# Storing the normed tokens in the order of the weight rows

## What is computed

```python
for i in range(2):
    hl = xl * (1 + sc1) + sh1
    yl = diff_attention(hl, ctx) if i == 0 else pool_mixer(hl)
    xl = layer_norm(ALPHA * xl + (1 + g1) * yl, ln_g[i, 0], ln_b[i, 0])
    tokens = xl * (1 + sc2) + sh2
    y2 = moe_ffn(tokens, router_w, router_b, wg[i], wu[i], wd[i])   # top 2 of 16 experts
    xl = layer_norm(ALPHA * xl + (1 + g2) * y2, ln_g[i, 1], ln_b[i, 1])
```

## Time and profile before

| | us |
|---|---|
| median of 3 runs | 1341.49 |
| lowest and highest | 1334.39 and 1345.14 |
| the profiled execution, its own time | 1343.82 |
| its span on the core | 1341.9 |
| PE busy | 1229.0 (92%) |
| mean granted TensorE clock | 0.971 |

### The profile page before, as it was taken

The page is one execution under the profiler, slowest core; times in us unless marked ns, Lnnn a source line. Parts: engine busy times, 40 slices in busy tenths (PEclk is TensorE's granted clock), DMA queues, the critical chain, the costliest instruction groups (busy, mean ns, idle before and its releaser), DMA issues.

```text
span 1341.9 us, 12310 instructions
## 1 busy us (share of the span) xinstructions
PE 1229.0 (92%) x5261; PEld 564.1 (42%) x5261; DVE 379.3 (28%) x781; ACT 166.5 (12%) x398; POOL 23.0 (2%) x28
## 2 busy tenths in 40 slices
PE   5999999988999999999999998899999999999996
PEld 1444344454644434444443435644444444444332
DVE  1486897854211111111111113311111111111103
ACT  0200123332201000000100002400100000010000
POOL 0011001000000000000000010000000000000000
PEclk8799899899899999999999999999999999999997
DMA  9668867606899999999999998299999999999950
GB/s 330 260 251 316 318 238 255 251 1 247 344 418 423 426 429 429 427 426 428 429 426 428 428 420 369 95 420 422 427 427 428 428 428 427 427 428 427 428 236 32
DMA packets 54924, 476.27 MB, mean 355 GB/s; under 512 B 5018, under 2 KB 6442, under 8 KB 30292
## 3 DMA queue, kind: packets, MB, share of 16 engines
q1 hardware_dynamic: 42632, 433.04, 77.3%
q0 software_dynamic: 10560, 41.94, 8.5%
q10 hardware_dynamic: 1676, 0.46, 0.3%
HBM read 474.38 MB, written 1.05 MB: 354 GB/s over the span
## 4 chain that ended last, share of the span: by engine, by line
PE 81%; DVE 10%; DMA 4%; issue 2%; ACT 2%; SPq 0%; DVEq 0%
PE ps L731 50%; PE ps L723 9%; PE ps L528 5%; PE ps L739 5%; DMA ring<-in_mod_w 4%; DVE modp L1150 3%; PE ps L593 2%; DVE work L1480 2%; DVE work L1484 2%; PE ps L747 1%; PE ps L557 1%; PE ps L501 1%; PE ps L575 1%; PE ps L682 1%; PE ps L451 1%
## 5 line engine op out<-in xcount | busy, mean ns | idle before, releaser
L731 PE MATMUL ps<-ring,tra 128*64 128x512 f32 x2048 | 446.5, 594 | 1.1 <-ACT tra L1032 1.1
L731 PEld LDWEIGHTS ps<-ring,tra 128*64 128x64 f32 x2048 | 146.1, 137 | 296.6 <-issue 295.1
L731 PE MATMUL ps<-ring,work 128*64 128x512 f32 x1024 | 228.5, 598 | 29.5 <-DVE work L1480 29.5
L731 PEld LDWEIGHTS ps<-ring,work 128*64 128x64 f32 x1024 | 83.3, 137 | 154.1 <-issue 117.9
L528 PE MATMUL ps<-ring 128*128 128x512 f32 x320 | 142.7, 599 | 0.7 <-ACT ring L921 0.7
L723 PEld LDWEIGHTS ps<-extra,xn 128*128 128x128 f32 x512 | 121.7, 328 | 25.7 <-issue 22.7
L723 PE MATMUL ps<-extra,xn 128*128 128x128 f32 x512 | 127.5, 405 | 2.7 <-DVE extra L1389 2.7
L1150 DVE SCALAR_TENSOR_TENSOR modp<-ring,modp 128x512 f32<-128x512 f32 x140 | 105.3, 752 | 5.0
L1475 DVE TENSOR_TENSOR work<-ps,work 128x512 f32<-128x512 f32 x32 | 22.1, 692 | 283.4 <-ACT work L1039 283.4
L528 PEld LDWEIGHTS ps<-ring 128*128 128x128 f32 x320 | 59.8, 192 | 78.1 <-issue 77.1
L739 PE MATMUL ps<-work,extra 64*128 64x512 f32 x256 | 63.6, 615 | 25.1 <-DVE work L1484 25.1
(11 more groups left out here) (177 smaller groups left out, 641.5 us busy)
## 6 DMA issues: line engine op xcount, KB each, us to landing
ring<-in_moe_wg SPq DMA_DIRECT2D x64, 2048.0 KB, 14.8
ring<-in_moe_wu SPq DMA_DIRECT2D x64, 2048.0 KB, 12.1
ring<-in_moe_wd SPq DMA_DIRECT2D x64, 2048.0 KB, 12.1
ring<-in_mod_w POOLq DMA_DIRECT2D x20, 2048.0 KB, 9.7
ring<-in_attn_wqkv SPq DMA_DIRECT2D x6, 2048.0 KB, 15.0
ring<-in_mod_w SPq DMA_DIRECT2D x4, 2048.0 KB, 18.6
ring<-in_attn_wo SPq DMA_DIRECT2D x2, 2048.0 KB, 9.0
xn<-in_x SPq DMA_DIRECT2D x1, 1024.0 KB, 17.0
```

The lines of the kernel that those rows point to most:

```text
L731: last = mm(ps[SLOTS * h:SLOTS * h + SLOTS, b, :], lhs(k0 + k), w[:, k, h * NB:(h + 1) * NB], start=(k0 + k == 0), stop=(k0 + k == KT - 1) ...
```

## The change

The normed tokens for norms 0 and 2 are stored in `xn` in the order of a unit's weight rows (`in_order`): within a half, all features 4f come first, then 4f + 1, and so on. A gather then reads 128 neighbouring columns. What else follows:

- norm 0 can't be done in place; the residual sum goes to `zbuf`, a piece of the ring's slot of unit 7, so SP's load of unit 7 waits for the norm instead of the sum;
- router weights are loaded in two transfers in the second order, and `bcol`, `acol`, `xcol` for the router and the residual use index 1;
- `open_sums` in the router (start=True) writes its 128 columns to every fourth column of the bank, which brings the sums back to the natural order; the one in the pool layer stays as it was;
- `route` on PE gets fillers: three after the second of its four turned parts and one after the last.

```diff
+        zbuf = [ring[:, e9:e9 + D], small9]
+        def in_order(n, to, src):
+            if n == 1:
+                return to, src
+            return to.rearrange("p (k f) -> p f k", k=4), src.rearrange("p (f k) -> p f k", k=4)
...
                 elif v == 7:
-                    sp.wait_ge(sem("gated"), 2 * TT)
+                    normed(sp, 0, 1)
...
             def open_sums(t, k, start):
-                return mm(bank(2 * t + k // 4, 0, P, k % 4 * P, k % 4 * P + P), xT8[:, k, t * P:t * P + P], ident,
-                          start=start and k % 4 == 0, stop=True, skip_group_check=True)
+                to = bank(2 * t + k // 4)
+                to = to.rearrange("p (f k) -> p k f", k=4) if start else to.rearrange("p (k f) -> p k f", k=4)
+                return mm(to[:, k % 4, :], xT8[:, k, t * P:t * P + P], ident, start=start and k % 4 == 0, stop=True,
+                          skip_group_check=True)
...
                     turn_blocks(NT_BANK[part], xn[:, t * D + b * NB:t * D + (b + 1) * NB]).then_inc(sem("nT_done"), 1)
+                    if part == 1:
+                        keep_clock(NT_BANK[2], 3)
+                keep_clock(0, 1)
...
-                        half = xn[:, t * D + b * NB:t * D + (b + 1) * NB].rearrange("p (f k) -> p k f", k=4)
-                        last = mm(bank(bk, 0, P, k * P, k * P + slots), half[:, k, :], sgat[:, t, 0:slots],
+                        c0 = t * D + b * NB + k * P
+                        last = mm(bank(bk, 0, P, k * P, k * P + slots), xn[:, c0:c0 + P], sgat[:, t, 0:slots],
...
-            load(rw[:, :].rearrange("p (k n) -> p k n", k=KT)[:, :, 0:NE], router_w.rearrange("(k p) n -> p k n", p=P), "router_loaded")
+            for b in range(2):
+                load(rw[:, P * b:P * b + P].rearrange("p (k n) -> p k n", k=4)[:, :, 0:NE],
+                     router_w[HALF * b:HALF * b + HALF, :].rearrange("(p k) n -> p k n", p=P), "router_loaded")
...
-                half = xn[:, t * D + h * NB:t * D + (h + 1) * NB]
-                nc.scalar.activation(half, half if n == 0 else bank(2 * t + h), ACT.Identity, bias=m_[:, 4:5],
-                                     scale=m_[:, 2:3]).then_inc(sem("norm_act"), 1)
+                src = zbuf[t][:, h * NB:(h + 1) * NB] if n == 0 else bank(2 * t + h)
+                to, src = in_order(n, xn[:, t * D + h * NB:t * D + (h + 1) * NB], src)
+                nc.scalar.activation(to, src, ACT.Identity, bias=m_[:, 4:5], scale=m_[:, 2:3]).then_inc(sem("norm_act"), 1)
```

More of the change, by code:

```diff
@@ L636, in job @@
                     pe.wait_ge(sem("cols_ready"), 1)
-                    pe.wait_ge(sem("router_loaded"), 32)
+                    pe.wait_ge(sem("router_loaded"), 48)
                     for layer in range(DEPTH):
@@ L640, in job @@
                             last = mm(bank(bk, 0, P, NE * layer, NE * layer + NE),
-                                      one(bcol[2 * layer], k).to_broadcast([P, P]), rw[:, 32 * k:32 * k + NE],
+                                      one(bcol[2 * layer], k, 1).to_broadcast([P, P]), rw[:, 32 * k:32 * k + NE],
                                       start=(k == 0), stop=(k == KT - 1), skip_group_check=True)
@@ L1255, in job_out @@
                         link(v_.tensor_tensor(bcol[n], bcol[n], sh_, ALU.add))
-                        v_.tensor_scalar(xcol[:, 0, n], g[:, 0], ALPHA, None, ALU.mult)
-                        link(v_.tensor_scalar(xcol[:, 1, n], b[:, 0], ALPHA, None, ALU.mult))
+                        s_ = 0 if n == 1 else 1
+                        v_.tensor_scalar(xcol[:, 0, n], g[:, s_], ALPHA, None, ALU.mult)
+                        link(v_.tensor_scalar(xcol[:, 1, n], b[:, s_], ALPHA, None, ALU.mult))
                     v_.tensor_scalar(flat, bcol[1][:, 0].rearrange("p q h -> p h q"), cst[:, C_FLAT:C_FLAT + 1], None,
                                      ALU.mult).then_inc(sem("cols_ready"), 1)
-                    dve.wait_ge(sem("router_loaded"), 32)
+                    dve.wait_ge(sem("router_loaded"), 48)
                     scaled_router(0)
                 else:
-                    dve.wait_ge(sem("router_loaded"), 32)
+                    dve.wait_ge(sem("router_loaded"), 48)
                     v_.tensor_tensor(rb[:, NE:3 * NE].rearrange("p (l e) -> p l e", l=2),
@@ L1271, in scaled_router @@
                 four = lambda a: a[:, :].rearrange("p (h q n) -> p h q n", h=2, q=4)
-                a_ = acol[2 * layer][:, 0].rearrange("p q h -> p h q").unsqueeze(3).to_broadcast([P, 2, 4, 32])
+                a_ = acol[2 * layer][:, 1].rearrange("p q h -> p h q").unsqueeze(3).to_broadcast([P, 2, 4, 32])
                 v_.tensor_tensor(four(rwa[layer]), four(rw), a_, ALU.mult).then_inc(sem("rw_ready"), 1)
@@ L1327, in norm @@
                 dve.wait_ge(sem("rstd_ready"), TT * n + 2)
-                v_.tensor_scalar(xn[:, D + NB:2 * D], src, m_[:, 0:1], m_[:, 2:3], ALU.subtract, ALU.mult)\
+                to, src = in_order(n, xn[:, D + NB:2 * D], src)
+                v_.tensor_scalar(to, src, m_[:, 0:1], m_[:, 2:3], ALU.subtract, ALU.mult)\
                     .then_inc(sem("norm_dve"), 1)
@@ L1335, in attention_norm @@
                         c0, c1 = h * NB, (h + 1) * NB
-                        z, y = xn[:, t * D + c0:t * D + c1], ybuf[:, c0:c1]
+                        x_, z, y = xn[:, t * D + c0:t * D + c1], zbuf[t][:, c0:c1], ybuf[:, c0:c1]
                         mixed(dve, t, h)
                         link(v_.tensor_tensor(y, bank(2 * t + h), gate1[:, c0:c1], ALU.mult))
-                        ins = v_.scalar_tensor_tensor(out=z, in0=z, scalar=ALPHA, in1=y, op0=ALU.mult, op1=ALU.add)
+                        ins = v_.scalar_tensor_tensor(out=z, in0=x_, scalar=ALPHA, in1=y, op0=ALU.mult, op1=ALU.add)
                         ins.then_inc(sem("gated"), 1)
@@ L1344, in attention_norm @@
                     deviation(0, t)
-                norm(0, xn[:, D + NB:2 * D])
+                norm(0, zbuf[1][:, NB:D])
             def sums_norm(n, ready):
```

## The result

The changed kernel takes 1288.6 us (median of four runs, 1287.9 to 1292.7) against 1343.2 us for the kernel before: a ratio of 0.961 [0.956, 0.966]. The prediction was 1284, with a range of 1272 to 1295. The same kernel, run again beside the last experiments, gave 1287.1 us (six runs, 1280.1 to 1291.2) and 0.959 [0.955, 0.962].

The account below looks back on a forecast made before the run. PE's chain of 29.32 us an expert was taken as the bound, with transfers 24 us a layer behind. PE alone would gain 60.3 us; waits for units cut this to 56.7, from 1341.5 to 1284, range 1272 to 1295.

Parts of the forecast that it names:

- router of layer 0, the clock: From logits to first gather in layer 0, added fillers keep the clock up: 2.6 us saved.
- half-gathers, 14 a layer: Half-gathers in the expert loop read contiguous weights at 118 ns each: 1.89 us instead of 3.93, 28.6 us a layer.
- first gathers, both layers: First gather of each layer, 32 instructions reading contiguous weights, about half at low clock: 2.5 us saved a layer.
- strided PSUM write, both: Residual sums in each router write PSUM with a step of four, at 213 ns each: 1.8 us lost a layer.
- norms, both: Norms stored with a step of 512 bytes slow ACT's halves: 0.3 us lost a layer, bounds nothing to 0.6.
- fillers in layer 1: In layer 1's router the added fillers delay PE, mostly hidden by ACT's table load: 0.3 us lost.
- waits for units, both layers: At each layer's end PE waits for its last ring unit: 1.5 us in layer 0, another 2.1 in layer 1.
- The transfers: Expert units land at 4.915 us each, 417.8 us for 85 a layer, using up the cushion, so both bounds meet.
- Rival 3: Expert unit transfers hold their old pace of 4.944 us or worse: 1289, or 1297 at 4.99; chance 0.12.
- Rival 5: Gathers get no faster, the address step not being the cause; clock and small costs remain: 1343; chance 0.05.
- Rival 6: In the expert loop PE's clock falls once it waits for weights: 1390 with five such experts; chance 0.03.
- Rival 4: Everything falls well: 111 ns gathers, warm first gathers, free PSUM writes, transfers at 4.89 us: 1273; chance 0.05.

Follow-up runs that it names:

- the control: The changed kernel run again with no edit: 1287.1 us (six runs), ratio 0.959 to the kernel before.
- experiment 2: The changed kernel without its added fillers: 1286.1 us (four runs), ratio 0.960 to the kernel before.
- experiment 3: The changed kernel with half of each expert unit loaded and the matmuls reading that half twice: 1281.8 us, ratio 0.954.
- experiment 10: The changed kernel again; with more fillers ahead of first gathers; and also with norms reordered on the read and attention fillers: 1287.1, 1281.1, 1280.0 us.
- experiment 5: The changed kernel with gathers reading their weights at a step of two fp32 values instead of one: 1284.6 us (one run).
- experiment 7: The changed kernel with open_sums in the pool layer too writing every fourth PSUM column: 1290.0 us (one run).
- experiment 8: The changed kernel with norms reading at a step of 16 bytes and storing in order, instead of storing at 512: 1290.2 us (one run).
- experiment 9: The kernel before with half the bytes of the expert weights loaded and each read twice by the matmuls: 1342.3 us (one run).
- experiment 4: The changed kernel gathering only one of the four blocks of features: 1282.3 us (four runs), ratio 0.956.
- experiment 6: The changed kernel with gathers reading their weights at a step of eight fp32 values instead of one: 1341.2 us (one run).
- the last version of experiment 10: The changed kernel with more router fillers, norms reordered on the read and three fillers in the attention: 1280.0 us (six runs), ratio 0.953.

## Why the prediction was right

The time was off by 4.6 us and the gain from the projection on by 0.3. The second is closer than its terms, of which some were off in both directions. Term by term, in us of gain (before to after, from the rows above and those of before):

| step | predicted | measured |
|---|---|---|
| router of layer 0, the clock | 2.6 | 2.6 |
| half-gathers, 14 a layer | 28.6 twice | 27.3 twice |
| first gathers, both layers | 5.0 | 1.05 + 1.2 = 2.3 |
| strided PSUM write, both | -3.6 | 0 |
| norms, both | -0.6 | -0.45 twice = -0.9 |
| fillers in layer 1 | -0.3 | -0.3 |
| waits for units, both layers | -3.6 | -1.5 - 1.2 = -2.7 |
| last down matmuls | 0 | 1.5 |
| sum | 56.7 | 57.1 (by the spans 57.0) |

**Half-gathers.** The mechanism was right, the price wrong by 6 ns: 124 ns an instruction, the higher of the two rows it was taken between the earlier trace rows, so 3.93 - 1.98 = 1.95 us each instead of 2.04. The row nearer in kind was the band matmuls, which read the same tile.

**First gathers.** These were over-priced. The prediction let half of each run cold; after, both ran nearly whole at 0.50, and their 6.70 and 6.54 us are close to the 6.8 us that it had worked out for that case. A window within layer 0's:

```profile
348.00:350.00 2.00, 2.00 (x11) 2.00 (x11) 0.61 (x6) 0.00 (x0) 0.00 (x0) 0.50 1.02 434
```

Other executions had 5.2 to 5.5 us in one layer or both (the control above, experiments 2 and 3), so half warm is seen too, and 3.84 in layer 1 of experiment 2. Experiment 10 takes what is left. The prediction let the clock in the first gather be as before, and priced the fillers for the stretch ahead of it only. In six traces with these fillers and no more (the changed kernel's two, experiments 3, 5, 7 and 8) both first gathers took over 5 us, and in the one trace without them layer 1's took 3.84. So the fillers may have a cost there that the sum doesn't have; one trace doesn't show it.

**The router's clock.** In layer 0 the added fillers did what the sum had them do. The logits of layer 0 take 1.11 us, in the chain after, where they took 1.98, and from them to the first gather it is 347.65 - 337.91 = 9.74 us instead of 12.33. In layer 1 it was 9.74 before and is 9.70 now. Their price there was right too: from layer 0's last scatter to layer 1's logits it is 28.65 us before, 29.10 without the fillers (experiment 2) and 29.40 with them. So 0.45 us are the norm's and 0.3 the fillers'.

**PSUM write.** Priced at 1.8 us a layer between bounds of 0 and 2.9; the lower bound is the truth (experiment 7). In layer 1, in the changed kernel, the 32 of them take the same 4.27 us as before:

```profile
821.58 4.27 PE L691 MATMUL ps<-cst,work 128*128 128x128 f32 x32
```

**Norms.** They cost 0.45 us a layer, between the 0.3 that was taken and the bound of 0.6: ACT's last half, which PE waits for, went from 0.8 us to 1.24 and 1.29 (experiment 8). In layer 0 this is the way from the projection to the logits, 20.57 us before and 21.04 after.

**The last down matmuls.** 7.26 us instead of 8.81, a gain of 1.5 us that no step foresaw. It isn't the change's: the kernel before had 7.11 in experiment 9, and the kernels of experiments 2 and 4, made from the changed one, had 8.78. The clock's fall there comes and goes between executions. Without it the gain in this pair of traces would have been 55.5 us.

**The transfers.** The step that decided the forecast held. The time of issue and the time to landing of layer 0's unit 10 (unit 95, issued at 745.4, is the 40.24 us in the chain above):

```profile
L356 SPq DMA_DIRECT2D ring<-in_moe_wd x1: 328/328/328, 358.8 to 358.8; - x1
DMA to landing us min/median/max: 7.7/7.7/7.7
```

Unit 10 lands at 366.5 and unit 95 at 785.65: 419.1 us for 85, 4.931 each. In layer 1 unit 107, issued at 840.3, lands 7.9 us later at 848.2, and unit 192, issued at 1226.8, lands 40.4 us later at 1267.2: 419.0 us, 4.929 each. The prediction had these four at 365.3, 783.1, 846.7 and 1264.5: each is 1.2 to 2.7 us later than that. But this execution reached its projection 1.5 us later than the one before (316.87 against 315.35); counted from there, they are within 0.3 us at the start of each layer, and 1.0 and 1.2 us late at its end. The forecast had 4.915, and the upper rival 4.944. PE lost 1.5 us in layer 0 and 1.2 in layer 1, against 1.5 and 2.1. These are the times by which the experts of a layer took longer than their own work; the idle times shown above are 1.04 and 1.03 us of them, and each break in a row of matmuls costs another 0.2 (two times sixteen take 3.65 + 3.65 us where 32 in a row take 7.09). **Rival 3** in its milder form is half true, at 0.015 us a unit.

Errors of some 6 us each way cancelled. The gathers gave 2.6 + 2.7 us less and the norms 0.3 less; the PSUM write, the last down matmuls and the waits gave 3.6 + 1.5 + 0.9 more. That the gain came out within 0.3 us is luck; that it lay near 57 is not. The prediction's structure also made it forgiving: where two bounds meet, an error on PE's side comes back in part as shorter or longer waits. Of the 4.6 us between 1284 and the median, 1.7 lie in the kernel before, whose median beside it was 1343.2 instead of 1341.5. The rest is that these medians differ by 54.7 us and the traces by 57.0 from the projection on; beside the control the medians differ by 56.4. That is within what executions differ by in their first 320 us (last section).

**Rival 5** (the step isn't the cause) is refuted by experiment 6, which puts the step back and with it the time. **Rival 6**, the fall of the clock in the expert loop, is seen inside the loop only in experiment 4 and decides nothing there; in a layer's last down matmuls it comes and goes in both kernels and costs 1.5 to 1.7 us each time. **Rival 4** asked for warm first gathers and free PSUM writes; experiment 10's versions have both and reach 1280, not 1273, for a gather's instruction takes 120 to 124 ns instead of 111 and the transfers stayed at 4.93 us a unit.

## What to carry to other kernels

When two places load weights of the same shape and one takes twice as long, compare their address steps: here fp32 weights cost 124 to 130 ns per 128 columns with at least two values in every 16 bytes and 246 to 250 with one, and the order of storing could be chosen for the reader, because only the norm, the router's weights and the residual had to follow. Before you price a faster engine, work out the cushion of the resource beside it, as the time between the landing of a layer's last unit and its use: a share of 1.0 for the transfers said nothing of it, the kernel before had 24 us a layer to give, and the change used them up. From there on neither side alone brings much: experiments 3 and 4 win 4.0 and 1.6 us for half the traffic or for 50 us less of work. And a filler that keeps the clock up in one stretch should be judged with the stretch behind it, for here the low clock turned up there.

## What the runs showed of the hardware that was not expected

**Executions differ ahead of the experts.** Over the kernels run here the measured stretch starts between 308.5 and 320.0 us, although the code before it is the same in nearly all of them, and the runs of one kernel spread over 5 to 11 us. From there on, the changed kernel's two traces differ by 1.3 us. The spread grows in steps: of two traces that end up 11.5 us apart (experiments 2 and 8) one is 4.8 us ahead at 55 us already and 6.8 at 250 us. Between 250 and 312 us it can be read from the clock, which is granted at 0.50 (1.2 GHz) for shorter or longer stretches. In the changed kernel, for example, in the attention:

```profile
264.00:267.00 3.00, 3.00 (x16) 2.60 (x16) 2.88 (x9) 0.00 (x0) 0.00 (x0) 0.50 0.00 0
```

and in the sixteen matmuls of the first output projection, in the control, in the last version of experiment 10, which has fillers ahead of them, and in experiment 7, which has none:

```profile
284.98 9.86 PE L600 MATMUL ps<-ring 128*128 128x512 f32 x16 [0.77 <-ACT ring L977]
```

```profile
285.55 7.11 PE L600 MATMUL ps<-ring 128*128 128x512 f32 x16 [0.82 <-ACT ring L987]
```

```profile
289.64 7.11 PE L600 MATMUL ps<-ring 128*128 128x512 f32 x16 [0.82 <-ACT ring L977]
```

PE is busy throughout the window and is granted half the clock all the same. Whether it is low in a given execution isn't set by the program alone; what else sets it stays open. For a change of a few us a stretch of the trace that begins after such a place tells more than the medians.

**Where a step is free and where not** (fp32, 128 partitions). A matmul's PSUM write (0.89 us for 8) and ACT's PSUM read (0.78 us for 512 columns) with a step of 16 bytes: free. Weights from SBUF with a step of 8 bytes: 130 ns an instruction instead of 124; of 16 or 32 bytes: 246 and 250. ACT on 512 columns of SBUF, read with a step of 16 bytes or written with 512: 1.27 to 1.30 us instead of 0.81.
